# The low halves of the weight units written by VectorE in four instructions of 512 columns instead of one of 2048, in a four-layer transformer trunk

## What is computed

```
for i in range(DEPTH):
    h = _rmsnorm(x, attn_norm[i])
    if i % 3 == 0:   x = x + stick_breaking_mixer(h, sb_w_qkv[j], sb_w_o[j])
    elif i % 3 == 1: x = x + mla_mixer(h, mla_w_down[j], ...)
    else:            x = x + swa_sink_mixer(h, swa_w_qkv[j], ...)
    h = _rmsnorm(x, ffn_norm[i])
    x = x + (silu(h @ w_gate) * (h @ w_up)) @ w_down
return _rmsnorm(x, final_norm)
```

## Time and profile before

| | |
|---|---|
| three runs | 1190.5, 1191.11, 1191.27 us; median 1191.11 us |
| the profiled execution, its own time | 1189.64 us |
| its span | 1187.8 us |
| instructions | 18200 |
| TensorE busy (matmul) | 1158.3 us, 98% |
| VectorE busy | 816.5 us, 69% |
| ScalarE busy | 625.4 us, 53% |
| GpSimd busy | 285.8 us, 24% |
| 16 DMA engines | 170 GB/s over the span |
| TensorE's granted clock | 0.996 of full speed |

### The profile page before, as it was taken

One profiled execution on the slowest core, in us unless ns is written; L12 is line 12 of the kernel. 1 busy time (PEld: TensorE's weight loads), 2 busy tenths in 40 slices (PEclk: granted clock), 3 DMA queues, 4 the chain that ended last, 5 costly groups with the idle time before them and its releaser, 6 DMA issues.

```text
span 1187.8 us, 18200 instructions
## 1 busy us (share of the span) xinstructions
PE 1158.3 (98%) x7410; PEld 1033.0 (87%) x7410; DVE 816.5 (69%) x865; ACT 625.4 (53%) x731; POOL 285.8 (24%) x290
## 2 busy tenths in 40 slices
PE   8999999999999999999999899999999999999996
PEld 6999888888998888888898888888889898888885
DVE  8686867675588667766558767766556767777653
ACT  5675555554354555555345655554346755555531
POOL 5000542211123353221111253221110005322221
PEclk9999999999999999999999999999999999999999
DMA  8733545555562345556544245556545335455541
GB/s 315 216 125 107 177 178 183 182 204 196 182 175 86 109 170 210 183 178 212 180 175 141 80 170 211 179 177 213 180 175 178 107 106 178 177 202 185 196 162 35
DMA packets 30828, 201.84 MB, mean 170 GB/s; under 512 B 3504, under 2 KB 4592, under 8 KB 7328
## 3 DMA queue, kind: packets, MB, share of 16 engines
q1 hardware_dynamic: 28800, 197.41, 47.3%
q0 software_dynamic: 352, 1.31, 0.9%
q10 hardware_dynamic: 1600, 2.02, 0.7%
HBM read 197.91 MB, written 1.84 MB: 168 GB/s over the span
## 4 chain that ended last, share of the span: by engine, by line
PE 88%; DVE 8%; ACT 2%; issue 0%; DMA 0%; POOL 0%; DVEq 0%; ACTq 0%
PE banks L1232 40%; PE banks L1236 21%; PE banks L1226 6%; PE banks L1228 5%; PE banks L1227 5%; PE banks L1220 4%; DVE w_lo L796 3%; DVE x_split L811 2%; PE banks L1361 1%; PE banks L1303 1%; ACT w_hi L465 1%; PE banks L1375 1%; DVE w_lo L805 1%; PE banks L1363 0%; ACT x_split L477 0%
## 5 line engine op out<-in xcount | busy, mean ns | idle before, releaser
L796 DVE TENSOR_TENSOR w_lo<-raw,w_hi 128x2048 fp32r<-128x2048 f32 x183 | 450.4, 2462 | 218.0 <-ACT w_hi L465 217.8
L465 ACT ACTIVATE w_hi<-raw 128x2048 fp32r<-128x2048 f32 x183 | 349.3, 1909 | 95.5 <-PE banks L1236 47.2
L1232 PE MATMUL banks<-x_split,w_hi 128*128 128x512 f32 x1408 | 338.9, 392 | 5.4 <-DVE x_split L811 5.4
L1232 PEld LDWEIGHTS banks<-x_split,w_hi 128*128 128x128 f32 x1408 | 258.4, 188 | 58.6 <-DVE x_split L811 8.9
L1236 PEld LDWEIGHTS banks<-x_split,w_lo 128*128 128x128 f32 x1408 | 180.5, 191 | 6.9
L1236 PE MATMUL banks<-x_split,w_lo 128*128 128x256 f32 x1408 | 182.6, 283 | 0.0
L1232 PE MATMUL banks<-hid_split,w_hi 128*128 128x512 f32 x704 | 173.1, 391 | 0.0
L1232 PEld LDWEIGHTS banks<-hid_split,w_hi 128*128 128x128 f32 x704 | 127.4, 188 | 23.3
L1226 PE MATMUL banks<-x_split,w_hi 128*128 128x256 f32 x384 | 110.5, 288 | 0.0
L1227 PE MATMUL banks<-x_split,w_hi 128*128 128x256 f32 x384 | 108.6, 283 | 0.0
L1228 PE MATMUL banks<-x_split,w_lo 128*128 128x256 f32 x384 | 108.6, 283 | 0.0
(11 more groups left out here) (174 smaller groups left out, 1458.6 us busy)
## 6 DMA issues: line engine op xcount, KB each, us to landing
raw<-w SPq DMA_DIRECT2D x183, 1024.0 KB, 4.9
raw<-w SPq DMA_DIRECT2D x8, 256.0 KB, 6.2
x<-x_in SPq DMA_DIRECT2D x2, 512.0 KB, 5.4
raw<-w SPq DMA_DIRECT2D x2, 512.0 KB, 8.5
out<-x SPq DMA_DIRECT2D x4, 256.0 KB, 2.8
k_all<-k_all ACTq DMA_DIRECT2D x1, 960.0 KB, 11.8
rel_scratch<-rel_lut POOLq DMA_DIRECT2D x1, 768.0 KB, 10.6
rel_bias<-rel_scratch POOLq DMA_DIRECT2D x2, 256.0 KB, 8.9
```

The lines of the kernel that those rows point to most:

```text
L465: act.activation(w_hi[slot][:, :], raw[slot][:, :], ACT.Copy).then_inc(hi_done, 1)
L796: dve.tensor_tensor(w_lo[slot][:, :], raw[slot][:, :], w_hi[slot][:, :].bitcast(FP32), ALU.subtract).then_inc(lo_done, 1)
L1232: return pe.matmul(pair(b), wt[0], xs, start=first, stop=False, skip_group_check=True)
```

## The change

`split(u)` on VectorE makes the low part in four instructions of 512 columns (`LOW_STEP`). They stand one behind the other with no wait between them, and the last one alone raises `lo_done`. The bytes read and written are the same, as are all waits and the order of everything else. VectorE gets 3 x 183 = 549 instructions more.

```
+LOW_STEP = 512

             def split(u):
...
                 slot = u % RAW_SLOTS
                 dve.wait_ge(hi_done, u + 1)
-                dve.tensor_tensor(w_lo[slot][:, :], raw[slot][:, :], w_hi[slot][:, :].bitcast(FP32),
-                                  ALU.subtract).then_inc(lo_done, 1)
+                for first in range(0, UNIT, LOW_STEP):
+                    cols = slice(first, first + LOW_STEP)
+                    ins = dve.tensor_tensor(w_lo[slot][:, cols], raw[slot][:, cols], w_hi[slot][:, cols].bitcast(FP32),
+                                            ALU.subtract)
+                ins.then_inc(lo_done, 1)
```

## The result

| | before | after |
|---|---|---|
| median of 5 runs | 1190.57 us (1189.20 to 1191.27) | 1197.77 us (1196.59 to 1198.04) |
| profiled execution, its span | 1189.64 us, 1187.8 us | 1198.04 us, 1196.2 us |
| TensorE busy (matmul) | 1158.3 us | 1164.3 us |
| VectorE busy | 816.5 us | 872.2 us |
| GpSimd busy | 285.8 us | 269.6 us |

The ratio is 1.0058, 95% interval 1.0047 to 1.0069: 0.6% slower, clear of no change, and in the direction that was forecast. The forecast was 1196.0 us, or 4.9 us more; it came to 7.2 us more.

What follows compares the result with a forecast made beforehand. TensorE, busy 1158.3 of 1187.8 us, was taken as the bound. Layers 0, 1, 3 (2.2), layer 2 (1.2), latent (0.95) and window attention (0.6) summed to 4.9 us: median 1196.0 us, range 1192.3 to 1202.0 us.

Steps and rivals of the forecast that it cites:

- Slower, by the fixed cost of more instructions: Whole kernel: instruction overhead on the chain of waits, GpSimd contention about as it is, 4.9 us slower; chance 0.60.
- Steps of layers 0, 1, 3 add 0.72 us each: Mixer-to-channel-mixer steps: three cut splits add 0.24 us each, all landing on TensorE; 2.2 us for the three layers.
- about the same: Layer steps: VectorE's loss to GpSimd stays near 2.67 us, six instructions, but moves from the norm_lo pairs into the splits.
- Step of layer 2, 1.2 us: Layer 2's mixer-to-channel-mixer step: 0.72 us for the pieces plus 0.47 us for one more GpSimd instruction let in.
- Channel mixers: nothing: Some 130 of the 183 units: no cost, since the low part is ready 5.6 us before TensorE needs it.
- one of the prediction's own signs of being wrong: Channel mixers: any appearing waits would show the forecast wrong; no TensorE wait for w_lo was expected there.
- Latent attention, 0.95 us: Two splits on the chain of waits at 0.24 us each, plus 0.47 us for a GpSimd scaling let in.
- Window attention 0.6 us: The split pair at 642.74 delays by 0.48 us and the split at 668.69 by 0.24.
- A gain from the lock: Four layer steps: GpSimd, no longer held for whole units, finishes early and spares VectorE; 1188.2 us, chance 0.06.
- No change: Whole kernel: pieces start closer together or fewer GpSimd instructions get in; about +1.5 us, 1192.6 us, chance 0.15.
- Strict alternation: Layer steps: every piece of the second and third splits meets a GpSimd instruction; 1202.5 us, chance 0.12.
- Pieces that don't overlap: Every split: each piece starts only when the one ahead has ended, 0.56 us more per unit; 1201.4 us, chance 0.07.

Runs made afterwards that it cites:

- experiment 5: The changed kernel with a semaphore wait between the pieces, each starting when the one ahead has ended: 1221.73 us, ratio 1.0263.
- experiments 2 and 4: First: kernel before, all splits cut except twelve in the mixer-to-channel-mixer steps, 1193.38 us. Second: changed kernel, last hidden low part before last split, 1196.65, repeated 1196.54 us.
- experiment 1: The kernel before with only the twelve splits of the four mixer-to-channel-mixer steps cut into four pieces: 1194.74 us, ratio 1.0029.
- 6 (two pieces): The changed kernel with two pieces of 1024 columns in every split: 1191.35 us, ratio 1.0007 to the kernel before.
- experiment 9: The changed kernel with each step's third split moved behind the last tile's norm_lo: 1189.68 us, ratio 0.9993 to the kernel before.
- experiment 8: The kernel before, uncut, with each step's third split moved behind the last tile's norm_lo: 1185.35 us, ratio 0.9952.

## Why the prediction was right, and where not

- **Slower, by the fixed cost of more instructions: right.** The mechanism and the sign held; 1197.77 us lies inside the range. That the places come to 5.15 us without the falls of the clock and the program's start, near the 4.9 that were forecast, is partly luck: the steps came out 0.6 us under, the latent and window attention 0.2 each, and the ends of the channel mixers, counted as nothing, 1.4 over. A piece costs 0.60 us from start to start (0.61 forecast), a unit 2.41 instead of 2.20. VectorE: DVE Perf Modes of the Trainium skill, section "The DRAIN you can't avoid", says that chaining without semaphores gains nothing, though it adds that some instructions start earlier; here the measurement decides: 0.60 us without waits, 0.70 with them (experiment 5).
- **"Steps of layers 0, 1, 3 add 0.72 us each": mis-sized.** They added 0.52: a unit costs 0.20 us more where 0.24 was put in, and VectorE loses 0.09 less to GpSimd. The four steps added 2.75 instead of 3.4. The total lost to GpSimd in layer 0, 1.38 in C and 0.72 and 0.48 in the two pairs, is 2.58 us against 2.67 before, so "about the same" held; the reason given, the supply of tiles, is argued and not shown. Where it is lost was wrong. The forecast let three GpSimd instructions in during B and three during C, with none left for the pairs. B lost nothing (the square was held for 3.19 us), C lost 1.38 (3.79 us against 2.41 for four pieces alone), and the pairs took 1.52 and 1.28 us, not 0.8. No square was to be held for 2.5 us; one was for 3.2.
- **Step of layer 2, 1.2 us: measured 1.18, by luck.** The forecast let GpSimd into B, and it was held over all of B as before. The extra came from C (3.79 instead of 2.64 us, less 0.37 in the pair behind it).
- **"Channel mixers: nothing": failed.** The cover of 5.6 us is that of `w_lo`. Behind the last split stands `hid_split`, with 0.07 us of cover, and TensorE needs it next. 4 x 0.34 = 1.4 us, which the prediction should have found by its own question of what is queued behind the instruction that grows (experiments 2 and 4). A wait in a channel mixer was one of the prediction's own signs of being wrong; the one for `w_lo` that it named did not come.
- **Latent attention, 0.95 us: near in size (0.7) by luck.** Ahead of the loop stand more splits than the one of the description, at 343.54, 350.68, 360.24 and 369.58 us. The first three, between which VectorE has next to no idle time, brought the 0.7 and were not in the sum. The two that were, at 369.67 (the fourth of these) and 382.26 in the earlier trace rows, cost VectorE 0.52 and 0.26 us (0.71 and 0.24 were forecast) and TensorE 0.6 against experiment 1; the hold-ups that went away by themselves hid it. I had read the chain of waits for the places, and it names one path only.
- **Window attention 0.6 us: measured 0.37**, 0.18 from the pair and 0.20 from the last split. Stick-breaking attention: 0, as said.
- **Not considered: the falls of the clock**, 1.5 us each, two in the profiled execution. Without them the offset ends at 5.4 us, of which 0.25 is the program's start; with them it is the 8.4 us of the two profiles.
- **VectorE's load.** Its busy time was to rise by about 40 us and its idle time ahead of the splits to fall by as much. They moved by 56 and by 20.
- **The rivals.** A gain from the lock: refuted by experiments 5 and 6 (two pieces), in which GpSimd is let in earlier and the step gets longer all the same. Only with C last (experiment 9) did an earlier GpSimd spare TensorE a wait, and that kernel is slower than the uncut one too. No change: outside the interval. Strict alternation: true of C alone. Pieces that don't overlap: refuted (0.60 us), and built in experiment 5.

## What to carry to other kernels

Cutting an instruction up on an in-order engine costs its fixed part wherever nothing idles behind it; look for the covers of all that is queued behind it, the short ones first, not only for that of its own result. If an engine does work for later ahead of work for now, moving it back (experiment 8, 4.0 us less in the trace and 5.6 in the medians) is worth more than making it finer. And small new stalls on a nearly full TensorE can cost more than their length, so a difference of some microseconds should be read at offsets by place before the total is believed.

## What the hardware showed unexpectedly

**A row of VectorE instructions without waits can keep GpSimd out.** The first square of a step starts 0.16 to 0.24 us ahead of B. In the six profiles with B in four pieces it was held for 3.13 to 3.20 us in all 24 steps, with eight pieces for 3.41 to 3.47 in all four. With a wait between the pieces it took 0.72 to 0.79 us in all four, and with B whole it took 0.72 to 0.79 in layers 0, 1 and 3 and was held (2.99) in layer 2 only. SBUF — State Buffer of the Trainium skill, section "SBUF: two separate sides", gives the lock to whoever starts first, for the whole instruction; these traces show it kept for a row of instructions, and by the listed starts GpSimd was the first each time and was the one held, so that a listed start need not be the moment at which the lock is taken. Yet an instruction that starts while the row is already running gets in behind the piece under way: in C (128.67, 1.06 us) and with two pieces in B (124.05, 1.48 us). Why the one that starts just ahead of the row fares worse, and why the length of the pieces matters to it, stays open.

**TensorE's clock fell behind short stalls, not always the same ones.** From 2.4 to 1.2 GHz, 1.5 us lost as a rule. In latent attention it fell behind the stall near 390 us in five profiles (stalls of 1.94, 1.94, 1.93, 1.80 and 2.30 us), held in three with stalls just as long (1.94, 1.93 and 2.21 us), and held in all five with stalls of 1.67 to 1.72 us. Behind waits of 0.19, 0.76 and 0.82 us in a step it fell in at most two of the four steps, which ones differing between executions (138, 426, 428, 692, 1000, 1002 and 1003 us, or none). So no length of stall in these runs decides it alone. TensorE: Matmul & The Clock Gate of the Trainium skill, section "Part 1: The HAM clock gate (the "warmup" mystery)", says that the chip's watch on TensorE's activity runs freely, not tied to the program's start. The groups of times 1.5 us apart, and falls that come or stay away behind the same stall, agree with that. The two kernels with C last and uncut, which have the shortest such stalls in the steps (one of 0.7 us at most), are also the ones whose runs scatter least.
